# Slab parts, output parts and the last head norm of a gated delta rule's preparation issued later, inside the inverse

## The chip, the cores and the metric

The kernel runs on one core of one Trainium2 chip. The metric is the device time of one execution in microseconds, the median of the runs. All data are fp32; the large projections split each operand into a high and a low fp32r part and add three products.

## The reference

Two blocks of two layers each over 512 tokens and a width of 1024. The change is in the gated delta rule of the first block's two layers (4 heads of 128, here in 4 blocks of 128 tokens):

```python
h = h + 0.5 * swiglu_ffn(rms_norm(h, ffn1_norm[l]), ...)
h = h + hybrid_mixer(...)            # stick-breaking heads beside delta-rule heads
h = h + memory_cross_attention(...)
h = h + 0.5 * swiglu_ffn(...)

# inside the delta rule
decay = where(tril_incl, exp(g[:, None] - g[None, :]), 0)
lower = where(strict, (k*beta) @ k.T * decay, 0)
sol   = triangular_solve(lower + eye, concat([v*beta, k*beta*exp(g)]))
u, w  = split(sol)
qk    = where(tril_incl, q @ k.T * decay, 0)
# scan over the blocks: v_new = u - w @ state; o = q_dec @ state + qk @ v_new; ...
```

The output of the stick-breaking heads is normed per head (`sb_out_norm`) and, beside the delta rule's output, is the input of the output projection.

## The kernel before

Work is a list of stages. Each engine has one program, written out by hand; engines meet only at semaphores. `Mixer` is the stage in question and runs twice, once in each layer of the first block. It has three stretches.

First, the stick-breaking heads in pairs, mixed with the projection slabs of the delta rule. A slab is a weight tile of 128x2048 that DMA brings to `slab_raw`; ScalarE rounds it to `slab_hi` (`k.high`, L277), VectorE takes the rest to `slab_lo` (`k.low`, L284). Head norms are "items": `square(j)` on ScalarE, `sum_item(j)` on TensorE (L1425), `log(j)` (L1671) and `root(j)` (L1676) on ScalarE with a table load ahead of each, `norm(j)` on VectorE (L1869). Item 11 is the norm of the last pair. `high(i)` (L1681, `x_hi`) and `low(i)` (L1875, `x_lo`) split the four output parts for the output projection.

Second, the preparation of the delta rule, a block of 128 tokens (c = 0 to 3) at a time:

- `tensor_rows(c)`: three groups of four matmuls: keys by queries (L1503), the row of gate sums (L1510), the row of betas (L1515).
- `vector_rows(c)`: k times beta (L1944), then the gate difference in four parts (L1949). `scalar_rows(c)`: two exponentials (L1768, L1770). GpSimd masks the decay (L1355).
- `tensor_products(c)`: keys and values turned (L1525, L1528), keys by k-beta (L1535). `scalar_keep(c)`: eight scaled copies of the turned keys, to `k_beta_g` and `k_to_end` (L1781). `vector_products(c)`: five instructions of 128x512 (L1963, L1964, L1966, L1968, L1971), the last makes `inverse_t`, called dt.
- `tensor_turn_d(c)` turns dt (L1544), `scalar_d(c)` copies it out (L1787).

Blocks use PSUM banks 4 to 7 and 0 to 3 by turns (`base(c)`), so `tensor_rows(c)` waits for the readers of block c-2.

Third, the inverse in six levels (`tensor_invert`, `vector_invert`), each for four blocks: first products (L1559), masked on VectorE (L1985); second products (L1565), subtracted on VectorE (L1989); but for the last level, turned again (L1572) and copied by ScalarE (`scalar_turned`, L1794). After it comes the scan over the blocks. Names that the queues below carry: `gdn_qkv` holds queries, keys and values, later the masked and turned matrices; `h_squares`/`gdn_z` are scratch and the gate.

Before the change ScalarE and VectorE have the slab's two parts, the four output parts and item 11 between the blocks of the preparation.

Of the kernel before, what the change touches and what calls it, by code (L numbers as in the profile page):

```python
# [12 lines left out]
P = 128  # L13
# [1208 lines left out]
class Mixer(Stage):  # L1222
# [95 lines left out]
    def item(self, j):  # L1318

        kind, n = ITEMS[j]  # L1320
        data = self.o[:, n, :] if kind == "o" else self.raw[:, (0 if kind == "q" else 4) + n, :]
        batch = [b.index(j) for b in self.BATCH if j in b]
        return data, self.squares[:, j % 6, :], self.k.ps[:, 3 + batch[0] if batch else 2, :]

# [36 lines left out]
    def tensor(self, pe):  # L1361
# [113 lines left out]
        for c in range(TB):  # L1475
            if c + 1 < TB:
                self.tensor_rows(pe, c + 1)
            self.tensor_products(pe, c)
            if c == 0:
                sum_item(11)  # L1480
            if c >= 1:
                self.tensor_turn_d(pe, c - 1)
        self.tensor_turn_d(pe, TB - 1)
        self.tensor_invert(pe)
        self.tensor_scan(pe)
# [33 lines left out]
    def tensor_products(self, pe, c):  # L1519
# [27 lines left out]
    def blocks(self, a, b, odd):  # L1547
        return a.rearrange("p (q two b) -> p q two b", two=2, b=b)[:, :, odd, :]

    def tensor_invert(self, pe):  # L1550
        nc, H = self.k.nc, GD_HEADS
        pe.wait_ge(*self.kept.at(TB))
        pe.wait_ge(*self.vb_kept.at(TB))
        pe.wait_ge(*self.dec_ready.at(TB))
        for n, b in enumerate(self.levels):
            for c in range(TB):
                pe.wait_ge(*self.d_copied.at(n * TB + (c if n else max(c, 2)) + 1))
                for h in range(H):
                    mm = nc.tensor.matmul(self.bank(4 + c)[:, h, :], self.lt[:, c * H + h, :], self.heads(0, c)[:, h, :],  # L1559
                                          start=True, stop=True)  # L1560
                mm.then_inc(self.m1_ready.sem, 1)
# [73 lines left out]
    def scalar(self, act):  # L1635
# [97 lines left out]
        self.scalar_rows(act, 2)  # L1733
        self.scalar_keep(act, 1)
        self.scalar_d(act, 0)
        high(3)
        self.scalar_rows(act, 3)
        self.scalar_keep(act, 2)
        self.scalar_d(act, 1)
        self.scalar_keep(act, 3)  # L1740
        self.scalar_d(act, 2)
        self.scalar_d(act, 3)
        self.scalar_turned(act, 0)
        nc.scalar.activation(self.z, self.z, ACT.Silu).then_inc(self.z_silu.sem, 1)
# [26 lines left out]

    def scalar_keep(self, act, c):
        nc, g = self.k.nc, self.gates
        keys, values, kk, kq = self.base(c)
        act.wait_ge(*self.turned.at(c + 1))
        if c == 0:
            act.wait_ge(*g.bg_ready.at(1))
        for to, bank, col in ((self.kbg, keys, g.bg), (self.kend, keys, g.kend)):
            for h in range(GD_HEADS):
                u = c * GD_HEADS + h  # L1780
                ins = nc.scalar.activation(to[:, u, :], self.bank(bank)[:, h, :], ACT.Copy, scale=col[:, u:u + 1])  # L1781
        ins.then_inc(self.kept.sem, 1)

# [14 lines left out]
    def vector(self, dve):  # L1798
# [130 lines left out]
        self.vector_rows(dve, 2)  # L1929
        self.vector_products(dve, 1)  # L1930
        norm(11)
        self.vector_rows(dve, 3)
        self.vector_products(dve, 2)
        low(2)
        self.vector_products(dve, 3)
        low(3)
        self.vector_invert(dve)
        self.vector_scan(dve)
# [33 lines left out]

    def vector_invert(self, dve):
        k, nc, H = self.k, self.k.nc, GD_HEADS
# [6 lines left out]
        for n, b in enumerate(self.levels):  # L1981
            mask = k.c("levels", (n + 1) * P, P).unsqueeze(1).broadcast_to([P, H, P])
            for c in range(TB):
                dve.wait_ge(*self.m1_ready.at(n * TB + c + 1))
                nc.vector.tensor_tensor(self.heads(4, c), self.bank(4 + c), mask, ALU.mult).then_inc(self.m1_masked.sem, 1)  # L1985
            for c in range(TB):
                dve.wait_ge(*self.p_ready.at(n * TB + c + 1))
                a = halves(self.of(self.dt, c), b, 1)
                nc.vector.tensor_tensor(a, a, close(self.bank(c), b), ALU.subtract).then_inc(self.updated.sem, 1)  # L1989
            if n in (3, 4):  # L1990
                dve.wait_ge(*self.mem_hi_ready.at(1))
                for c in range(4 * n - 12, 4 * n - 8):
                    ins = nc.vector.scalar_tensor_tensor(out=self.mem_lo[:, c, :], in0=self.mem[:, c, :],
                                                         scalar=self.mem_gain[:, c:c + 1],
                                                         in1=self.mem_hi[:, c, :].bitcast(F32),
                                                         op0=ALU.mult, op1=ALU.subtract)
        ins.then_inc(self.mem_split.sem, 1)

# [904 lines left out]
```

## Time and profile before

| | us |
|---|---|
| median of 3 runs | 3319.66 (3318.96 to 3319.77) |
| the profiled execution | 3322.68 |
| its span | 3320.6 |
| PE busy | 3257.4 (98%) |
| PE weight loads busy | 2683.8 (81%) |
| DVE busy | 1664.3 (50%) |
| ACT busy | 1342.0 (40%) |
| POOL busy | 147.4 (4%) |

PE is TensorE, DVE VectorE, ACT ScalarE, POOL GpSimd, SP the engine that issues the DMAs. Each fp32 matmul stands in the trace as two records, so four matmuls of the program read x8. Matmul records overlap: a group's cost in a stream is the distance from its start to the next group's start. "idle ... <-" names what ended the wait. A mixer's preparation lies near 590 to 622 us in the first layer and near 1853 to 1885 us in the second.

### The profile page before, as it was taken

How to read it: one execution, taken by the hardware profiler on the slowest of the kernel's cores; microseconds unless marked ns; L12 is line 12 of the kernel's file. 1: busy time of each engine (PE TensorE's matmuls, PEld its weight loads, DVE VectorE, ACT ScalarE, POOL GpSimd, SP SyncE). 2: the span in 40 equal slices, each digit the busy share in tenths (PEclk: the TensorE clock that was granted, in tenths of full speed). 3: DMA queues.
4: the chain of work that ended last, by engine and by line, in shares of the span. 5: the costliest groups of instructions: out<-in, count | busy, mean ns of one | idle time of the engine just before them, and what ended most of it. 6: DMA issues, size and time to landing. Idle time of an engine off the chain costs nothing.

```text
span 3320.6 us, 39177 instructions
## 1 busy us (share of the span) xinstructions
PE 3257.4 (98%) x16640; PEld 2683.8 (81%) x16640; DVE 1664.3 (50%) x2280; ACT 1342.0 (40%) x1735; POOL 147.4 (4%) x176
## 2 busy tenths in 40 slices
PE   8999999899999999999999899999999999999999
PEld 7888887898688888888887798688888886888767
DVE  5443358654544434443348655444434457543574
ACT  5222248533432223222338643332224446453463
POOL 0000001100000000000001200000000004000040
PEclk9999999999999999999999999999999999999999
DMA  4222221022122222222221113122222220222102
GB/s 162 100 94 90 99 83 55 26 91 100 51 91 100 90 96 106 91 100 88 103 77 64 39 54 112 51 102 90 97 91 107 77 79 24 75 97 89 64 21 88
DMA packets 46893, 275.03 MB, mean 83 GB/s; under 512 B 5248, under 2 KB 8576, under 8 KB 21504
## 3 DMA queue, kind: packets, MB, share of 16 engines
q1 hardware_dynamic: 46720, 272.53, 23.0%
q8 instruction: 132, 2.16, 0.3%
q14 instruction: 41, 0.34, 0.0%
HBM read 270.41 MB, written 2.10 MB: 82 GB/s over the span
## 4 chain that ended last, share of the span: by engine, by line
PE 93%; DVE 3%; ACT 2%; issue 1%; DMA 0%; SPq 0%; ACTq 0%; DVEq 0%
PE banks L295 78%; PE banks L1559 1%; PE banks L1389 1%; PE banks L2747 1%; PE banks L1565 1%; PE banks L2418 1%; PE banks L2430 1%; PE banks L2216 1%; PE banks L1002 1%; ACT slab_hi L277 1%; DVE slab_lo L284 1%; PE banks L1425 1%; PE banks L1572 1%; PE banks L1086 0%; PE banks L1374 0%
## 5 line engine op out<-in xcount | busy, mean ns | idle before, releaser
L295 PE MATMUL banks<-x_hi,slab_hi 128*128 128x512 f32 x2688 | 1061.1, 395 | 12.0 <-DVE x_lo L376 11.6
L295 PE MATMUL banks<-x_hi,slab_lo 128*128 128x512 f32 x2688 | 1048.4, 390 | 0.0
L295 PE MATMUL banks<-x_lo,slab_hi 128*128 128x512 f32 x2688 | 1048.0, 390 | 0.0
L277 ACT ACTIVATE slab_hi<-slab_raw 128x2048 fp32r<-128x2048 f32 (+2 forms) x276 | 483.7, 1753 | 1037.3 <-PE banks L295 1024.1
L284 DVE TENSOR_TENSOR slab_lo<-slab_raw,slab_hi 128x2048 fp32r<-128x2048 f32 (+2 forms) x276 | 577.3, 2092 | 425.1 <-ACT slab_hi L277 425.1
L295 PEld LDWEIGHTS banks<-x_hi,slab_hi 128*128 128x128 f32 x2688 | 505.4, 188 | 123.4 <-issue 18.7
L295 PEld LDWEIGHTS banks<-x_lo,slab_hi 128*128 128x128 f32 x2688 | 505.5, 188 | 108.9 <-issue 5.7
L295 PEld LDWEIGHTS banks<-x_hi,slab_lo 128*128 128x128 f32 x2688 | 505.1, 188 | 105.7
L295 PE MATMUL banks<-hidden_hi,slab_lo 128*128 128x512 f32 x704 | 274.2, 389 | 0.0
L295 PE MATMUL banks<-hidden_hi,slab_hi 128*128 128x512 f32 x704 | 274.2, 389 | 0.0
L295 PE MATMUL banks<-hidden_lo,slab_hi 128*128 128x512 f32 x704 | 274.2, 389 | 0.0
L801 DVE TENSOR_TENSOR hidden<-banks,rstd 128x512 f32<-128x512 f32 x88 | 60.8, 690 | 313.9 <-PE banks L295 313.9
L778 DVE SCALAR_TENSOR_TENSOR h<-banks,h 128x512 f32<-128x512 f32 x80 | 55.1, 689 | 217.8 <-PE banks L295 217.8
L810 ACT ACTIVATE hidden_hi<-hidden 128x512 fp32r<-128x512 f32 x88 | 55.6, 632 | 255.2 <-DVE hidden L818 255.2
L295 PEld LDWEIGHTS banks<-hidden_lo,slab_hi 128*128 128x128 f32 x704 | 132.2, 188 | 27.5
L295 PEld LDWEIGHTS banks<-hidden_hi,slab_hi 128*128 128x128 f32 x704 | 132.2, 188 | 27.4
L295 PEld LDWEIGHTS banks<-hidden_hi,slab_lo 128*128 128x128 f32 x704 | 132.2, 188 | 27.3
L295 PE MATMUL banks<-slab_hi,x_hi 128*128 128x256 f32 x384 | 112.4, 293 | 0.0
L295 PE MATMUL banks<-slab_hi,x_lo 128*128 128x256 f32 x384 | 108.8, 283 | 0.0
L295 PE MATMUL banks<-slab_lo,x_hi 128*128 128x256 f32 x384 | 108.8, 283 | 0.0
L2454 POOL TENSOR_SCALAR weights<-weights,row_scale 128x128 f32<-128x128 f32 (+1 forms) x64 | 85.5, 1341 | 480.2 <-DVE row_scale L2513 480.2
L807 ACT ACTIVATE silu_gate<-silu_gate 128x512 f32<-128x512 f32 x88 | 55.7, 632 | 117.8 <-DVE silu_gate L801 117.7
(362 smaller groups left out, 3984.0 us busy)
## 6 DMA issues: line engine op xcount, KB each, us to landing
slab_raw<-slabs SPq DMA_DIRECT2D x196, 1024.0 KB, 4.8
slab_raw<-slabs SPq DMA_DIRECT2D x64, 704.0 KB, 4.0
slab_raw<-slabs SPq DMA_DIRECT2D x16, 640.0 KB, 3.9
h<-xT SPq DMA_DIRECT2D x8, 256.0 KB, 5.6
memory<-memT SPq DMA_DIRECT2D x2, 1024.0 KB, 5.2
out<-h SPq DMA_DIRECT2D x8, 256.0 KB, 4.3
constants<-con SPq DMA_DIRECT2D x1, 1412.5 KB, 10.2
memory_in<-memT SPq DMA_DIRECT2D x1, 1024.0 KB, 14.6
```

What stands on the lines that cost most here:

```text
L277: self.nc.scalar.activation(self.wh[:, g % self.HIGHS, 0:w], self.raw[:, g % self.RAWS, 0:w], ACT.Copy).then_inc(self.hi_ready, 1)
L284: self.nc.vector.tensor_tensor(self.wl[:, g % self.RAWS, 0:w], self.raw[:, g % self.RAWS, 0:w], self.wh[:, g % self.HIGHS, 0:w].bitcast(F3 ...
L295: mm = self.nc.tensor.matmul(out, left[a], right[c], start=start and n == 0, stop=stop and n == 2)
L778: k.nc.vector.scalar_tensor_tensor(out=h, in0=k.ps[:, jobs[n].bank, :], scalar=self.scale, in1=h, op0=ALU.mult, op1=ALU.add).then_inc(k.ba ...
L801: k.nc.vector.tensor_tensor(to, k.ps[:, jobs[n].bank, :], k.rstd[:], ALU.mult).then_inc(k.bank_free, 1)
L807: k.nc.scalar.activation(a, a, ACT.Silu).then_inc(k.act_done, 1)
L810: k.nc.scalar.activation(self.hh[:, i, :], self.hid[:, i % 2, :], ACT.Copy).then_inc(k.hh_ready, 1)
L1002: mm = nc.tensor.matmul(ps[:, 4 + c, :], self.k.c("heads64"), self.buf(p)[:, c, :], start=True, stop=True)
L1389: mm = nc.tensor.matmul(sc[:, to:to + n], (self.tail if j == b else self.full)[:], part[:, at:at + n], start=False, stop=True, skip_group_ ...
L1425: nc.tensor.matmul(bank, k.c("heads64") if ITEMS[j][0] == "o" else k.ones[:], sq, start=True, stop=True) \
L1559: mm = nc.tensor.matmul(self.bank(4 + c)[:, h, :], self.lt[:, c * H + h, :], self.heads(0, c)[:, h, :], start=True, stop=True)
L2454: ins = self.k.nc.gpsimd.tensor_scalar(w, w, self.col(self.ri, tb, 1), None, ALU.mult)
```

## The change

On ScalarE and VectorE the slab's parts, the four output parts and item 11 move out of the preparation to places in the inverse's first two levels (VectorE's inverse is cut into calls by level for this). On TensorE item 11's sum moves from behind block 0's products to behind the first products of level 0; level 0's first products of blocks 0 and 1 come before the fourth block's dt is turned, with waits of their own by bank. On ScalarE `scalar_keep` is cut in two, with a copy of the previous block's dt between the halves, and each block's exponentials come after the previous block's copies.

The end of the preparation on TensorE, where L1544 turns a dt and L1559 are the first products of level 0. Before:

```order
L1535 MATMUL banks<-k_beta,gdn_qkv 128x128 x4
L1544 MATMUL banks<-constants,inverse_t 128x128 x4
L1525 MATMUL banks<-constants,gdn_qkv 128x128 x4
L1528 MATMUL banks<-constants,gdn_qkv 128x128 x4
L1535 MATMUL banks<-k_beta,gdn_qkv 128x128 x4
L1544 MATMUL banks<-constants,inverse_t 128x128 x8
L1559 MATMUL banks<-gdn_qkv,l_transposed 128x128 x16
L1565 MATMUL banks<-inverse_t,gdn_qkv 128x64 x16
```

After (L1546 turns, L1565 are first products, L1582 second products, L1425 is item 11's sum):

```order
L1537 MATMUL banks<-k_beta,gdn_qkv 128x128 x4
L1546 MATMUL banks<-constants,inverse_t 128x128 x4
L1565 MATMUL banks<-gdn_qkv,l_transposed 128x128 x8
L1546 MATMUL banks<-constants,inverse_t 128x128 x4
L1565 MATMUL banks<-gdn_qkv,l_transposed 128x128 x8
L1425 MATMUL banks<-head_squares,constants 128x512
L1582 MATMUL banks<-inverse_t,gdn_qkv 128x64 x16
```

Eight first products now stand ahead of the last turn, and the sum of item 11 behind the other eight.

VectorE from block 0's rows on, before:

```order
L1880 COPY sb_out<-banks 128x512
L284 TENSOR_TENSOR slab_lo<-slab_raw,slab_hi 128x2048
L1944 TENSOR_TENSOR k_beta<-banks,gdn_qkv 128x512
L1949 TENSOR_SCALAR decay<-banks,gdn_gc 128x128 x4
L1963 TENSOR_TENSOR l_transposed<-banks,decay 128x512
L1964 TENSOR_TENSOR decay<-banks,decay 128x512
L1966 TENSOR_TENSOR inverse_t<-l_transposed,constants 128x512
L1968 TENSOR_TENSOR v_beta<-banks,gdn_beta 128x512
L1971 TENSOR_TENSOR inverse_t<-constants,inverse_t 128x512
L1875 TENSOR_TENSOR x_lo<-sb_out,x_hi 128x512 x2
L1944 TENSOR_TENSOR k_beta<-banks,gdn_qkv 128x512
```

And after, in the first two levels of the inverse (L2003 masks, L2007 subtracts):

```order
L2003 TENSOR_TENSOR gdn_qkv<-banks,constants 128x4x128 x4
L2007 TENSOR_TENSOR inverse_t<-inverse_t,banks 128x128x2 x4
L1889 SCALAR_TENSOR_TENSOR sb_out<-sb_out,params,head_squares 128x512
L1895 TENSOR_TENSOR x_lo<-sb_out,x_hi 128x512 x3
L2003 TENSOR_TENSOR gdn_qkv<-banks,constants 128x4x128 x4
L2007 TENSOR_TENSOR inverse_t<-inverse_t,banks 128x64x4 x4
L1895 TENSOR_TENSOR x_lo<-sb_out,x_hi 128x512
L284 TENSOR_TENSOR slab_lo<-slab_raw,slab_hi 128x2048
L2003 TENSOR_TENSOR gdn_qkv<-banks,constants 128x4x128 x4
```

All that stood between the blocks on VectorE now stands behind level 0 and level 1.

ScalarE after, from the last block's copies to the third level (L1800 are the scaled copies, L1807 copies dt, L1814 the turned matrices, L1763 is the gate):

```order
L1800 ACTIVATE k_to_end<-banks,gdn_kend 128x128 x4
L1682 ACTIVATE head_squares<-sb_out 128x512
L1807 ACTIVATE gdn_qkv<-banks 128x4x128
L1688 ACT_TABLE_LOAD
L1688 ACTIVATE head_squares<-banks 128x512
L1693 ACT_TABLE_LOAD
L1693 ACTIVATE head_squares<-head_squares 128x512
L1698 ACTIVATE x_hi<-sb_out 128x512 x3
L1814 ACTIVATE gdn_qkv<-banks 128x4x128 x4
L1698 ACTIVATE x_hi<-sb_out 128x512
L277 ACTIVATE slab_hi<-slab_raw 128x2048
L1763 ACT_TABLE_LOAD
```

Three output parts, item 11's two table loads and its two functions now stand ahead of level 0's four turned copies, the slab's high part behind them.

The diff, cut to its core (`vector_invert` is otherwise the same code for one level n):

```diff
 # tensor
             self.tensor_products(pe, c)
-            if c == 0:
-                sum_item(11)
             if c >= 1:
                 self.tensor_turn_d(pe, c - 1)
+        for c in range(2):
+            self.tensor_off_diagonal(pe, 0, c)
         self.tensor_turn_d(pe, TB - 1)
+        for c in range(2, TB):
+            self.tensor_off_diagonal(pe, 0, c)
+        pe.wait_ge(*self.dec_ready.at(TB))
+        sum_item(11)
         self.tensor_invert(pe)
 # tensor_products
-        if c == 1:
-            pe.wait_ge(*self.logged.at(12))
-        elif c >= 2:
+        if c >= 2:
             pe.wait_ge(*self.d_copied.at(c - 1))
+    def tensor_off_diagonal(self, pe, n, c):
+        if n == 0 and c == 0:
+            pe.wait_ge(*self.kept.at(3))
+        elif n == 0 and c == 1:
+            pe.wait_ge(*self.vb_kept.at(3))
+        elif n == 0 and c == 2:
+            pe.wait_ge(*self.d_copied.at(3))
+        elif n == 0:
+            pe.wait_ge(*self.dec_ready.at(3))
+        pe.wait_ge(*self.d_copied.at(n * TB + c + 1))
+        for h in range(GD_HEADS):
+            mm = self.k.nc.tensor.matmul(self.bank(4 + c)[:, h, :], self.lt[:, c * GD_HEADS + h, :],
+                                         self.heads(0, c)[:, h, :], start=True, stop=True)
+        mm.then_inc(self.m1_ready.sem, 1)
 # tensor_invert
-        pe.wait_ge(*self.kept.at(TB))
-        pe.wait_ge(*self.vb_kept.at(TB))
-        pe.wait_ge(*self.dec_ready.at(TB))
                 pe.wait_ge(*self.m1_masked.at(n * TB + c + 1))
+                if n == 0 and c < 2:
+                    pe.wait_ge(*(self.kept, self.vb_kept)[c].at(TB))
+                elif n == 0:
+                    pe.wait_ge(*(self.d_copied.at(TB) if c == 2 else self.logged.at(12)))
 # scalar
         self.scalar_rows(act, 0)
-        for i in range(2):
-            high(i)
+        self.scalar_rows(act, 1)
+        for c in range(2):
+            self.scalar_keep(act, c, 0)
+            self.scalar_keep(act, c, 1)
+            if c:
+                self.scalar_d(act, 0)
+            self.scalar_rows(act, c + 2)
+        self.scalar_keep(act, 2, 0)
+        self.scalar_d(act, 1)
+        self.scalar_keep(act, 2, 1)
+        self.scalar_keep(act, 3, 0)
+        self.scalar_d(act, 2)
+        self.scalar_keep(act, 3, 1)
         square(11)
-        k.high(act, self.g0 + SB_HEADS + 1)
-        high(2)
-        self.scalar_rows(act, 1)
-        self.scalar_keep(act, 0)
+        self.scalar_d(act, 3)
         log(11)
         root(11)
...
+        for i in range(3):
+            high(i)
+        self.scalar_turned(act, 0)
         high(3)
...
+        k.high(act, self.g0 + SB_HEADS + 1)
 # vector
-        k.low(dve, self.g0 + SB_HEADS + 1)
-        self.vector_rows(dve, 1)
-        self.vector_products(dve, 0)
-        for i in range(2):
-            low(i)
...
+        for c in range(TB):
+            if c + 1 < TB:
+                self.vector_rows(dve, c + 1)
+            self.vector_products(dve, c)
+        self.vector_invert(dve, 0)
+        norm(11)
+        for i in range(3):
+            low(i)
+        self.vector_invert(dve, 1)
+        low(3)
+        k.low(dve, self.g0 + SB_HEADS + 1)
+        for n in range(2, len(self.levels)):
+            self.vector_invert(dve, n)
```

## Rows read from the trace of the kernel before

**Rows 1.** The page, part 4: the chain that ended last, shares of the span.
```profile
PE 93%; DVE 3%; ACT 2%; issue 1%; DMA 0%; SPq 0%; ACTq 0%; DVEq 0%
```

**Rows 2.** Windows, preparations: length, PE, PEld, DVE, ACT, POOL busy, PEclk, DMA, GB/s.
```profile
590.50:622.00 31.50, 22.09 (x157) 20.23 (x156) 23.49 (x42) 21.63 (x52) 10.37 (x19) 0.86 0.10 34
1853.50:1885.00 31.50, 22.09 (x156) 20.22 (x156) 23.49 (x42) 21.59 (x52) 10.37 (x19) 0.86 0.10 34
```

**Rows 3.** Timeline, TensorE, first mixer: start us, us, what, [idle before <- releaser].
```profile
592.38 1.06 PE L1515 MATMUL banks<-constants,gdn_beta 128*128 128x128 f32 x8
...
599.25 1.85 PE L1503 MATMUL banks<-gdn_qkv 128*128 128x128 f32 x8 [3.19 <-DVE decay L1964]
600.89 1.96 PE L1510 MATMUL banks<-constants,gate_g 128*128 128x128 f32 x8
602.65 1.20 PE L1515 MATMUL banks<-constants,gdn_beta 128*128 128x128 f32 x8
...
607.47 1.16 PE L1503 MATMUL banks<-gdn_qkv 128*128 128x128 f32 x8 [1.42 <-DVE decay L1964]
...
616.07 1.62 PE L1535 MATMUL banks<-k_beta,gdn_qkv 128*128 128x128 f32 x8 [1.95 <-ACT gdn_qkv L1787]
...
621.03 1.09 PE L1544 MATMUL banks<-constants,inverse_t 128*128 128x128 f32 x4 [2.49 <-DVE inverse_t L1971]
621.91 6.09 PE L1559 MATMUL banks<-gdn_qkv,l_transposed 128*128 128x128 f32 x32
627.84 3.69 PE L1565 MATMUL banks<-inverse_t,gdn_qkv 128*128 128x64 f32 x32
631.36 1.91 PE L1572 MATMUL banks<-constants,inverse_t 128*128 128x128 f32 x16
633.11 3.74 PE L1559 MATMUL banks<-gdn_qkv,l_transposed 128*128 128x128 f32 x32
...
636.68 3.69 PE L1565 MATMUL banks<-inverse_t,gdn_qkv 128*128 128x64 f32 x32
```

**Rows 4.** Timeline, VectorE, the same stretch.
```profile
594.07 2.29 DVE L284 TENSOR_TENSOR slab_lo<-slab_raw,slab_hi 128x2048 fp32r<-128x2048 f32 x1 [2.77 <-ACT slab_hi L277]
596.28 0.68 DVE L1944 TENSOR_TENSOR k_beta<-banks,gdn_qkv 128x512 f32<-128x512 f32 x1
596.89 1.11 DVE L1949 TENSOR_SCALAR decay<-banks,gdn_gc 128x128 f32<-128x128 f32 x4
...
603.89 0.69 DVE L1944 TENSOR_TENSOR k_beta<-banks,gdn_qkv 128x512 f32<-128x512 f32 x1 [1.67 <-PE banks L1515]
...
611.09 0.69 DVE L1944 TENSOR_TENSOR k_beta<-banks,gdn_qkv 128x512 f32<-128x512 f32 x1 [1.19 <-PE banks L1515]
...
617.80 0.69 DVE L1963 TENSOR_TENSOR l_transposed<-banks,decay 128x512 f32<-128x512 f32 x1 [1.13 <-PE banks L1535]
```

**Rows 5.** Timeline, ScalarE, the same stretch.
```profile
592.15 1.89 ACT L277 ACTIVATE slab_hi<-slab_raw 128x2048 fp32r<-128x2048 f32 x1
...
602.65 1.28 ACT L1676 ACT_TABLE_LOAD   x1
603.95 0.63 ACT L1676 ACTIVATE head_squares<-head_squares 128x512 f32<-128x512 f32 x1
...
606.79 1.12 ACT L1781 ACTIVATE k_beta_g<-banks,gdn_bg 128x128 f32<-128x128 f32 x4
607.79 1.15 ACT L1781 ACTIVATE k_to_end<-banks,gdn_kend 128x128 f32<-128x128 f32 x4
...
632.00 2.06 ACT L1794 ACTIVATE gdn_qkv<-banks 128x512 f32<-128x512 f32 x4 [9.24 <-PE banks L1572]
```

**Rows 6.** Windows in the first preparation, columns as in rows 2.
```profile
599.30:603.00 3.70, 3.70 (x18) 3.70 (x19) 2.92 (x5) 3.65 (x9) 0.91 (x2) 0.54 0.00 0
...
607.00:611.00 4.00, 3.16 (x26) 2.97 (x27) 2.90 (x5) 3.50 (x11) 1.43 (x4) 1.00 0.00 0
...
621.00:628.00 7.00, 6.96 (x38) 7.00 (x39) 2.56 (x4) 0.60 (x1) 0.00 (x0) 0.58 0.01 2
```

More of the change, by code:

```diff
@@ L1322, in item @@
         batch = [b.index(j) for b in self.BATCH if j in b]
-        return data, self.squares[:, j % 6, :], self.k.ps[:, 3 + batch[0] if batch else 2, :]
+        return data, self.squares[:, j % 6, :], self.k.ps[:, 3 + batch[0] if batch else 3, :]
     def head(self, a, c):
@@ L1548, in blocks @@
         return a.rearrange("p (q two b) -> p q two b", two=2, b=b)[:, :, odd, :]
+    def tensor_off_diagonal(self, pe, n, c):
[12 more added lines that the diff above has]
+        mm.then_inc(self.m1_ready.sem, 1)
     def tensor_invert(self, pe):
         nc, H = self.k.nc, GD_HEADS
-        pe.wait_ge(*self.kept.at(TB))
-        pe.wait_ge(*self.vb_kept.at(TB))
-        pe.wait_ge(*self.dec_ready.at(TB))
         for n, b in enumerate(self.levels):
             for c in range(TB):
[L1557 to L1561, printed above, removed]
+                if n:
+                    self.tensor_off_diagonal(pe, n, c)
             for c in range(TB):
                 pe.wait_ge(*self.m1_masked.at(n * TB + c + 1))
+                if n == 0 and c < 2:
+                    pe.wait_ge(*(self.kept, self.vb_kept)[c].at(TB))
+                elif n == 0:
+                    pe.wait_ge(*(self.d_copied.at(TB) if c == 2 else self.logged.at(12)))
                 for h in range(H):
@@ L1770, in scalar_rows, with scalar_keep @@
         nc.scalar.activation(self.of(self.dec, c), self.of(self.dec, c), ACT.Exp).then_inc(self.dec_exp.sem, 1)
-    def scalar_keep(self, act, c):
+    def scalar_keep(self, act, c, part):
         nc, g = self.k.nc, self.gates
-        keys, values, kk, kq = self.base(c)
         act.wait_ge(*self.turned.at(c + 1))
-        if c == 0:
+        if c == 0 and part == 0:
             act.wait_ge(*g.bg_ready.at(1))
[L1778 to L1782, printed above, removed]
+        to, col = (self.kend, g.kend) if part else (self.kbg, g.bg)
+        for h in range(GD_HEADS):
+            u = c * GD_HEADS + h
+            ins = nc.scalar.activation(to[:, u, :], self.bank(self.base(c)[0])[:, h, :], ACT.Copy, scale=col[:, u:u + 1])
+        if part:
+            ins.then_inc(self.kept.sem, 1)
     def scalar_d(self, act, c):
@@ L1923, in vector @@
         copy_out(self.PAIRS - 1)
-        k.low(dve, self.g0 + SB_HEADS + 1)
-        self.vector_rows(dve, 1)
-        self.vector_products(dve, 0)
-        for i in range(2):
-            low(i)
[L1929 to L1937, printed above, removed]
+        for c in range(TB):
[8 more added lines that the diff above has]
+        low(3)
+        k.low(dve, self.g0 + SB_HEADS + 1)
+        for n in range(2, len(self.levels)):
+            self.vector_invert(dve, n)
         self.vector_scan(dve)
@@ L1971, in vector_products, with vector_invert @@
         nc.vector.tensor_tensor(dt, ident, dt, ALU.subtract).then_inc(self.dt_ready.sem, 1)
-    def vector_invert(self, dve):
-        k, nc, H = self.k, self.k.nc, GD_HEADS
+    def vector_invert(self, dve, n):
+        k, nc, H, b = self.k, self.k.nc, GD_HEADS, self.levels[n]
         def halves(a, b, odd):
@@ L1980, in close @@
             return a[:, :, 0:P // 2].rearrange("p h (q b) -> p h q b", b=b)
[L1981 to L1996, printed above, removed]
@@ L1997, in vector_invert @@
-        ins.then_inc(self.mem_split.sem, 1)
+        mask = k.c("levels", (n + 1) * P, P).unsqueeze(1).broadcast_to([P, H, P])
+        for c in range(TB):
+            dve.wait_ge(*self.m1_ready.at(n * TB + c + 1))
+            nc.vector.tensor_tensor(self.heads(4, c), self.bank(4 + c), mask, ALU.mult).then_inc(self.m1_masked.sem, 1)
+        for c in range(TB):
+            dve.wait_ge(*self.p_ready.at(n * TB + c + 1))
+            a = halves(self.of(self.dt, c), b, 1)
+            nc.vector.tensor_tensor(a, a, close(self.bank(c), b), ALU.subtract).then_inc(self.updated.sem, 1)
@@ new lines, in vector_invert @@
+        if n in (3, 4):
+            dve.wait_ge(*self.mem_hi_ready.at(1))
+            for c in range(4 * n - 12, 4 * n - 8):
+                ins = nc.vector.scalar_tensor_tensor(out=self.mem_lo[:, c, :], in0=self.mem[:, c, :],
+                                                     scalar=self.mem_gain[:, c:c + 1],
+                                                     in1=self.mem_hi[:, c, :].bitcast(F32),
+                                                     op0=ALU.mult, op1=ALU.subtract)
+            if n == 4:
+                ins.then_inc(self.mem_split.sem, 1)
```

10 lines of the change are left out of this document (removed).

## The prediction

> **What bounds the kernel now.** I read the chain of waits first, then busy time by stretch, then the timelines of the three engines side by side. The chain is TensorE for 93% of the span [rows 1], so over most of the kernel only less or faster TensorE work would help. The two preparations are different: in each 31.50 us stretch PE is busy 22.09 us, DVE 23.49, ACT 21.61, none of them full, and the mean granted clock is 0.86 [rows 2]. The two stretches agree to 0.05 us in every column, so I work out the first and count it twice.
>
> The timelines say what the time goes to. PE stands still 3.19, 1.42, 1.95 and 2.49 us, released by DVE or ACT each time [rows 3]. DVE in turn waits for PE, and once 2.77 us for `slab_hi`, after which `slab_lo` takes 2.29 us, and only then does block 1's k-beta start, at 596.28 [rows 4]; PE had its input ready at 592.38 + 1.06 = 593.44 [rows 3]. It is a ring: rows on PE, k-beta and difference on DVE, exponential and scaled copies on ACT, and the banks given back to PE. What stands in the ring beside the blocks' own work is paid in full. The inverse is the opposite: from one level's second products to the next's it takes 636.68 - 627.84 = 8.84 us, made of first products 3.57, second 3.52 and turns 1.75, PE without a gap [rows 3].
>
> The clock is a second loss. After the 3.19 us stop the groups L1503 and L1510 take 1.64 and 1.76 us (599.25 to 600.89 to 602.65), where a group of four 128x128 takes 0.89 in the inverse (3.57/4); the stretch has 0.54 of the clock, near the 1.2 GHz level. Level 0's first products take 5.93 us (621.91 to 627.84) against 3.57 in level 1, at 0.58 [rows 3, 6]. Around the 1.42 us stop the clock stayed at 1.00, the 2.4 GHz level [rows 3, 6].
>
> **The change, term by term, for one mixer.** Nothing is removed but waits. I follow the starts of k-beta (L1944) on DVE.
>
> Term 1, the slab's two parts leave the way to block 1: k-beta goes from 596.28 to 593.44 less a hand-over, -2.9 us.
>
> Term 2, the ring from block 1 to block 2 is now k-beta 0.6 (596.28 to 596.89), difference 1.11 [rows 4], exponential 0.54 (its like is at 603.95, 0.63 long), eight scaled copies 1.00 + 1.15 (606.79, 607.79) [rows 5], PE's two row groups 0.89 + 1.06 [rows 3], five hand-overs of some 0.05: 6.6 us. Before it was 603.89 - 596.28 = 7.61 [rows 4], with item 11's loads and functions in ACT's part and 2.96 instead of 1.96 us for the row groups at the low clock (600.89 to 603.85). -1.0 us.
>
> Term 3, block 2 to block 3: the same 6.6 instead of 611.09 - 603.89 = 7.20. -0.6 us.
>
> Term 4, block 3's k-beta to level 0's second products. Before: 611.09 to 627.84, 16.75 us. Now: (a) k-beta by keys, L1535, waits for dt 1's copy, which stands one group of scaled copies earlier, so it starts 4.0 instead of 4.98 us after k-beta (616.07 - 611.09): -1.0. (b) L1535 at the high clock takes 1.1 instead of the 1.73 us that pass to DVE's L1963 at 617.80: -0.7. (c) DVE's five instructions to the turn's start keep their 3.2 us (617.80 to 621.03). (d) Then 6.81 us passed (621.03 to 627.84): the turn 0.88 and sixteen first products 5.93. Eight of these now fill PE's wait for dt 3; behind it remain the turn 0.44, eight products 1.78 and item 11's sum. The sum has the columns of one group of four (128x512), 0.89, the value I take; it was hidden in a stop of PE before and is now on the path. 3.1 instead of 6.81: -3.7. Together -5.4.
>
> The sum is -9.9 us per mixer, level 0's second products at about 617.9 on the old scale. Two mixers: -19.8.
>
> Where the moved work goes. ACT stood idle 9.24 us before level 0's turned copies at 632.00 [rows 5]. Ahead of them now stand two loads 1.28 each, log 0.60, root 0.63 and three parts at 0.54: 5.4 us. The log cannot start before the sum, about 618.0. That gives root's end at 620.9, the parts' end at 622.5 and the first copy finished at 623.1, against level 1's first products at 617.9 + 3.52 + 1.75 = 623.2. It fits, with 0.1 us to spare, so this is the place to watch. Banks: the last second products wait for the log, done near 618.7, needed at 620.6. Behind the copies come one part 0.54, slab part 1.9 [rows 5] and the gate's load and pass, 3.2 together (1.28 and, being 128x2048 like the slab, 1.9), to about 630.1; level 1's copies are wanted at 631. It fits by about 1 us. DVE has eight instructions per level of at most 128x512; at 0.61 each (596.28 to 596.89) that is at most 4.9 of 8.84 us [rows 4]. Level 0 adds the norm and three parts, four times 0.6, 2.4; level 1 adds 0.6 and 2.29. The first mask can be taken up from 0.9 us after the level's first product and must be done, 0.7 long, by 3.57: it may start 1.9 us late, and what comes between the last subtraction and that point, some 2 us of turns and first product, is free before. Both hide, so 0; if they did not, 5.3 us per mixer. POOL and the DMA queue are passed by nothing: the memory's load on SP still hangs on the fourth block's turned values, which come earlier.
>
> A price that the trace bears on directly is the table load. The row shows 1.28 us and the next activation 0.02 us behind it (602.65 + 1.28 to 603.95) [rows 5]. The Trainium skill, "ScalarE: Activation LUTs", section "What ACT_TABLE_LOAD costs", says a switch costs some 1.38 us more for a drain. By that, two switches would put ACT's copies 2.8 us later and the whole 2.7 us later a mixer, 5.3 for both; by the row, nothing. The row decides.
>
> Bounds. A sum at 0.44, if its second pass overlapped, would give 0.9 us back for both mixers; hand-overs and the ends of pipelined groups are read to about 0.1 us in some 12 steps a mixer, so the gain could be up to 1.2 us a mixer larger: low end 3299.9 - 0.9 - 2.4 = 3296.6.
>
> The profiled execution has 3322.68 us, 2.1 above its span and 3.0 above the median of 3319.66. From it: 3302.9. From the median, which I forecast: 3299.9.
>
> **Rivals.**
>
> Cold first stretch. The clock is the assumption. New stops of PE, by my steps: about 1.5 and 0.6 us before block 2's rows (about 595 to 598), 1.1 and 0.6 before block 3's, 1.2 before the last L1535, 1.1 before the last turn. The longest is close to the 1.42 us stop that kept the clock, but the 1.95 us one was followed by slow groups [rows 3, 6]. If the clock falls at block 2's rows the ring there costs 1.0 to 1.4 us as before: +2.4 for both, 3302.3. For it: the first two stops lie within about 3 us; against: all are shorter than 1.95.
>
> Cold to the end. If PE runs all of the preparation's slow places slowly again, terms 2, 4b and 4d lose 1.0, 0.7 and 2.8 us: +4.5 a mixer, 3308.9.
>
> ACT late in the inverse. If ACT's queue ahead of the turned copies is over 0.1 us longer than I have it, level 1 waits by the excess, and the gate's pass can do the same to level 2. A delay like one more load (1.28) in each: +2.6 for one level, +5.2 for both: 3302.5 to 3305.1. By the drain that the Trainium skill's page on ScalarE states it would be 3305.2.
>
> Only the first stall goes. If the ring is held by something that I take for hidden (GpSimd's mask, say) the blocks keep their 7.6 and 7.2 and term 4 its length: 2 x 2.9, 3313.9. Against: DVE waited for PE or ACT there, never for GpSimd. This is also the case in which the change does little of what it says.
>
> Slower. The inverse is the one stretch in which PE never stops. If no moved work hides there, ACT's 5.4 + 0.54 + 1.9 = 7.8 and DVE's 5.3 us are added in full, 13.1 against 9.9 gained: +3.2 a mixer, 3326.1. It decides from the point where ACT's late copies hold level 1 and DVE's slab part holds level 2, one after the other, for more than 9.9 us. Against: 9.24 us idle on ACT, at least 3.9 a level on DVE.
>
> **How the numbers follow.** All warm and hidden 50%, 3299.9 (own range 3296.6 to 3302). Cold first stretch 20%, 3302.3. Cold to the end 12%, 3308.9. ACT late 12%, 3302.5 to 3305.1. First stall only 4%, 3313.9. Slower 2%. Range: from the low bound to the cold case, 3296.6 to 3308.9, which leaves out half of that case and the last two. About 0.2%, 6.6 us, is what a measurement can tell from no change; only the last two fall short of it: faster 94%, same 4%, slower 2%.
>
> **What would show it.** In the new profile: block 1's k-beta about 5 us after block 0's; the three k-betas 6.6 us apart; no row group over 1.1 us; PE's stops four to six of at most 1.5 us; granted clock 1.00 from 595 us on; sixteen first products in two parts with the last turn between; level 0's second products 25.5 us after block 1's row of betas starts (592.38 before, 617.9 by my steps) and level 1's first products without a stop before them; 8.84 us per level throughout. It would be wrong if a level is longer, if PE waits for L1814's copies, or if the clock row shows 0.5 after 595.

## The result and the profile after

The changed kernel takes 3302.25 us (median of 5, 3301.78 to 3304.35) against 3319.77 us: ratio 0.9946, interval 0.9931 to 0.9960. Forecast were 3299.9 us, a range of 3296.6 to 3308.9, and faster. The profiled execution spans 3300.5 us (3302.44 us with what lies around it) against 3320.6.

Parts 1 and 4 of the page of the changed kernel, TensorE's busy time and the chain; TensorE is busy 11.2 us less though it does the same products:

```profile
PE 3246.2 (98%) x16640; PEld 2674.5 (81%) x16640; DVE 1663.8 (50%) x2280; ACT 1342.0 (41%) x1735; POOL 145.3 (4%) x176
...
PE 94%; DVE 3%; ACT 2%; issue 1%; DMA 0%; SPq 0%; DVEq 0%; ACTq 0%
```

The stretches that answer to [rows 2], columns as there (the second mixer starts 8.5 us earlier now):

```profile
590.50:622.00 31.50, 26.81 (x223) 24.48 (x219) 22.36 (x45) 18.83 (x49) 9.33 (x20) 1.00 0.11 36
1843.50:1875.00 31.50, 26.80 (x221) 24.27 (x217) 22.66 (x46) 18.42 (x48) 9.73 (x20) 1.00 0.13 43
```

The granted clock is 1.00 instead of 0.86, and PE is busy 4.7 us more of the same 31.50 us: since the preparation is shorter, the window now takes in more of the inverse. The timeline of TensorE that answers to [rows 3]; L1507, L1514 and L1519 are the old L1503, L1510 and L1515, and L1537, L1546, L1565, L1582, L1589 the old L1535, L1544, L1559, L1565, L1572:

```profile
591.50 1.16 PE L1507 MATMUL banks<-gdn_qkv 128*128 128x128 f32 x8
...
597.65 1.16 PE L1507 MATMUL banks<-gdn_qkv 128*128 128x128 f32 x8 [1.44 <-DVE decay L1983]
599.01 1.13 PE L1514 MATMUL banks<-constants,gate_g 128*128 128x128 f32 x8 [0.21 <-ACT k_to_end L1800]
...
604.25 1.16 PE L1507 MATMUL banks<-gdn_qkv 128*128 128x128 f32 x8 [1.01 <-DVE decay L1983]
605.60 1.13 PE L1514 MATMUL banks<-constants,gate_g 128*128 128x128 f32 x8 [0.20 <-ACT k_to_end L1800]
...
611.62 1.16 PE L1537 MATMUL banks<-k_beta,gdn_qkv 128*128 128x128 f32 x8 [0.92 <-ACT gdn_qkv L1807]
612.80 0.63 PE L1546 MATMUL banks<-constants,inverse_t 128*128 128x128 f32 x4
613.26 1.95 PE L1565 MATMUL banks<-gdn_qkv,l_transposed 128*128 128x128 f32 x16
616.12 0.63 PE L1546 MATMUL banks<-constants,inverse_t 128*128 128x128 f32 x4 [0.91 <-DVE inverse_t L1990]
616.58 2.07 PE L1565 MATMUL banks<-gdn_qkv,l_transposed 128*128 128x128 f32 x16
618.49 1.02 PE L1425 MATMUL banks<-head_squares,constants 128*128 128x512 f32 x2
619.35 3.68 PE L1582 MATMUL banks<-inverse_t,gdn_qkv 128*128 128x64 f32 x32
622.87 1.92 PE L1589 MATMUL banks<-constants,inverse_t 128*128 128x128 f32 x16
624.62 3.74 PE L1565 MATMUL banks<-gdn_qkv,l_transposed 128*128 128x128 f32 x32
628.19 3.68 PE L1582 MATMUL banks<-inverse_t,gdn_qkv 128*128 128x64 f32 x32
```

Six stops of at most 1.44 us stand where [rows 3] have four of 1.42 to 3.19; the prediction had 1.5, 0.6, 1.1, 0.6, 1.2 and 1.1, and they came as 1.44, 0.21, 1.01, 0.20, 0.92 and 0.91. No group is slow: L1507 and L1514 start 1.36 us apart with a stop between them. VectorE, answering to [rows 4]:

```profile
594.48 0.69 DVE L1963 TENSOR_TENSOR k_beta<-banks,gdn_qkv 128x512 f32<-128x512 f32 x1 [2.17 <-PE banks L1519]
...
601.07 0.69 DVE L1963 TENSOR_TENSOR k_beta<-banks,gdn_qkv 128x512 f32<-128x512 f32 x1 [1.61 <-PE banks L1519]
...
607.66 0.69 DVE L1963 TENSOR_TENSOR k_beta<-banks,gdn_qkv 128x512 f32<-128x512 f32 x1 [1.61 <-PE banks L1519]
...
612.88 0.69 DVE L1982 TENSOR_TENSOR l_transposed<-banks,decay 128x512 f32<-128x512 f32 x1 [0.23 <-PE banks L1537]
...
625.88 1.43 DVE L2003 TENSOR_TENSOR gdn_qkv<-banks,constants 128x512 f32<-128x512 f32 x2
...
635.06 1.98 DVE L2003 TENSOR_TENSOR gdn_qkv<-banks,constants 128x512 f32<-128x512 f32 x3
```

The k-betas (L1963) stand 6.59 us apart both times. Behind the moved norm and output parts VectorE takes up level 1's masks (L2003) at 625.88, behind the slab's low part those of level 2 at 635.06. TensorE's second products start at 628.19 and 637.04 all the same, 8.84 and 8.85 us after the level before: the moved work is hidden. ScalarE, answering to [rows 5]:

```profile
617.40 1.28 ACT L1688 ACT_TABLE_LOAD   x1
619.55 0.60 ACT L1688 ACTIVATE head_squares<-banks 128x512 f32<-128x512 f32 x1 [0.87 <-PE banks L1425]
620.16 1.28 ACT L1693 ACT_TABLE_LOAD   x1
621.46 0.63 ACT L1693 ACTIVATE head_squares<-head_squares 128x512 f32<-128x512 f32 x1
622.00 1.66 ACT L1698 ACTIVATE x_hi<-sb_out 128x512 fp32r<-128x512 f32 x3
623.56 2.04 ACT L1814 ACTIVATE gdn_qkv<-banks 128x512 f32<-128x512 f32 x4
...
632.36 2.06 ACT L1814 ACTIVATE gdn_qkv<-banks 128x512 f32<-128x512 f32 x4 [1.22 <-PE banks L1589]
```

The second table load ends at 621.44 and the root starts at 621.46. Level 0's turned copies (L1814) start at 623.56 and level 1's first products at 624.62, which is where TensorE's turns end: nothing waits.

From here on "the stretch" is the time from TensorE's first group behind the last pair's product of weights and values (L1404; the group starts at 590.49 us before, 591.50 after) to level 1's first products (633.11 and 624.62). Each is read from one profiled execution, to 0.02 us; whole executions of one kernel differ by up to 6.5 us.

| kernel | stretch, mixer 1 and 2 | span less both | median | ratio to before (interval) |
|---|---|---|---|---|
| before | 42.62, 42.63 | 3235.4 | 3319.77 | |
| changed | 33.12, 33.13 | 3234.3 | 3302.25 | 0.9946 (0.9931 to 0.9960) |
| slab parts only | 39.65, 38.19 | 3236.9 | 3316.40 | 0.9987 (0.9977 to 0.9996) |
| changed, slab back | 35.98, 35.93 | 3235.5 | 3309.20 | 0.9965 (0.9952 to 0.9978) |
| changed, turn first | 36.42, 36.12 | 3232.8 | 3307.61 | 0.9962 (0.9947 to 0.9977) |
| changed, item 11 back | 35.53, 35.39 | 3233.1 | 3305.97 | 0.9957 (0.9940 to 0.9973) |
| before with fillers | 39.74, 40.76 | 3234.4 | 3317.77 | 0.9993 (0.9984 to 1.0002) |
| changed, copies uncut | 34.17, 34.17 | 3235.5 | 3305.90 | 0.9952 (0.9939 to 0.9966) |
| sum early | 32.28, 32.28 | 3234.8 | 3301.27 | 0.9937 (0.9924 to 0.9951) |
| ring shortened | 30.95, 30.95 | 3235.4 | 3299.01 | 0.9930 (0.9917 to 0.9942) |
| values first | 29.31, 29.32 | 3233.7 | 3294.39 | 0.9925 (0.9913 to 0.9938) |
| changed, again | 33.12, 33.13 | 3233.8 | 3304.12 | 0.9951 (0.9937 to 0.9965) |

Each ratio is against before on the same chip, whose medians were 3319.74 to 3321.71 (single executions 3317.97 to 3323.23).

### The profile page after: what moved, and what is told of

Its sections match the earlier page's. It is cut to its first block, busy times and chain, and to the rows that moved or that the text cites. A ratio compares the mean times of both kernels' runs of the same rounds, so it can differ in the third digit from the quotient of the medians.

```text
span 3300.5 us, 39191 instructions
## 1 busy us (share of the span) xinstructions
PE 3246.2 (98%) x16640; PEld 2674.5 (81%) x16640; DVE 1663.8 (50%) x2280; ACT 1342.0 (41%) x1735; POOL 145.3 (4%) x176
## 4 chain that ended last, share of the span: by engine, by line
PE 94%; DVE 3%; ACT 2%; issue 1%; DMA 0%; SPq 0%; DVEq 0%; ACTq 0%
PE banks L295 78%; PE banks L1389 1%; PE banks L1582 1%; PE banks L2437 1%; PE banks L1565 1%; PE banks L2449 1%; PE banks L2766 1%; PE banks L2235 1%; PE banks L1002 1%; PE banks L1425 1%; ACT slab_hi L277 1%; DVE slab_lo L284 1%; PE banks L1404 1%; PE banks L1589 1%; PE banks L1086 0%
```

## The experiments

**Slab parts only.** In the kernel before:

```diff
         square(11)
-        k.high(act, self.g0 + SB_HEADS + 1)
 ...
         self.scalar_turned(act, 0)
+        k.high(act, self.g0 + SB_HEADS + 1)
 # vector: k.low(...) from ahead of vector_rows(dve, 1) to behind level 1
```

> The kernel before, with only the slab's two parts moved into the inverse; output parts, item 11, the order of turns and the uncut scaled copies stay. Theory (ring and clock): block 1's k-beta comes 2.9 us earlier in each mixer, TensorE's 3.19 us stop shrinks to about 0.4, the granted clock stays 1.00 at block 2's rows and they take 1.0 us less on the path; the later stops and the slow first products of level 0 stay. -3.9 us per mixer, -7.8 in all against before. Rival A (only the clock counts, the moved work was hidden anyway): -1.0 per mixer, -2.0. Rival B (only the moved work counts): -2.9 per mixer, -5.8, with the clock still at half after 599 us.

Measured -3.0 and -4.4 us a mixer. The first stop fell to 0.58 us and block 2's rows ran fast, as the theory said. But that gained nothing on the path: block 3's rows start 14.17 us into the stretch in both mixers, 2.81 earlier than before, which is what block 1's k-beta gained alone. The next stop grew from 1.42 to 2.44 us instead, and in the first mixer the clock fell there. TensorE at block 3's rows:

```profile
604.37 1.21 PE L1503 MATMUL banks<-gdn_qkv 128*128 128x128 f32 x8 [2.44 <-DVE decay L1967]
605.89 2.07 PE L1510 MATMUL banks<-constants,gate_g 128*128 128x128 f32 x8 [0.31 <-ACT k_to_end L1781]
607.76 1.54 PE L1515 MATMUL banks<-constants,gdn_beta 128*128 128x128 f32 x8
609.13 0.60 PE L1525 MATMUL banks<-constants,gdn_qkv 128*128 128x128 f32 x4
```

The row groups, 0.9 us each elsewhere, take 1.87 and 1.37 us; in the second mixer of the same execution they take 0.9. One program, two lengths of the same stretch: behind the same 2.44 us stop the clock fell once and held once. The theory's -3.9 lies between the two mixers, but not by its sum: the 1.0 us at block 2's rows is not in it, and level 0's first products took 4.87 and 4.67 us instead of 5.93. Rival B's -2.9 is the first mixer's number by chance, since its condition (slow rows behind 599 us) did not hold; rival A's -1.0 is out.

**The slab back in the changed kernel.** `k.high` ahead of block 1's exponentials, `k.low` ahead of block 1's rows, out of the inverse.

> The changed kernel with the slab's two parts back between block 0 and block 1, all else as changed. Theory: block 1's k-beta 2.9 us later, TensorE's stop before block 2's rows 1.4 + 2.9 = 4.3 us, so that the clock falls there and adds 1.0: +3.9 us per mixer, +7.8 against the changed kernel, -10 against before. Rival A (only the clock counts): +1.0 per mixer. Rival B (clock stays up): +2.9 per mixer, +5.8.

Measured +2.86 and +2.80. The stop grew to 2.48 us, not 4.3: ScalarE comes to the slab 0.09 us into the stretch, 1.57 earlier than in the kernel before, where two output parts and item 11's square stand ahead of it. Block 1's k-beta starts at 4.23 us instead of 2.98. The clock did fall behind the stop:

```profile
597.97 1.16 PE L1507 MATMUL banks<-gdn_qkv 128*128 128x128 f32 x8 [2.48 <-DVE decay L1983]
599.49 1.72 PE L1514 MATMUL banks<-constants,gate_g 128*128 128x128 f32 x8 [0.37 <-ACT k_to_end L1800]
601.00 1.92 PE L1519 MATMUL banks<-constants,gdn_beta 128*128 128x128 f32 x8
602.71 0.91 PE L1529 MATMUL banks<-constants,gdn_qkv 128*128 128x128 f32 x4
```

1.51 and 1.71 us for groups of 0.97 and 0.89. So both parts of the theory are there, with other sizes: the work 1.25 us where I had 2.9, the clock 1.36 where I had 1.0, and 0.24 in the next turn of the ring.

**Turn first.**

```diff
-        for c in range(2):
-            self.tensor_off_diagonal(pe, 0, c)
         self.tensor_turn_d(pe, TB - 1)
-        for c in range(2, TB):
+        for c in range(TB):
             self.tensor_off_diagonal(pe, 0, c)
```

> The changed kernel with all sixteen first products of level 0 behind the fourth block's turn. The stop before that turn grows from 0.9 to 2.9 us. Theory: eight products (1.8 us) return to the path, and after such a stop the clock falls as before, so that the first products take 5.9 instead of 3.6 us and the turn 0.4 more: +4.5 us per mixer, +9 against the changed kernel. Rival (the clock holds, since the earlier stops are short now): +1.8 per mixer, +3.6.

Measured +3.30 and +2.99, between the two. TensorE there:

```profile
614.91 0.63 PE L1544 MATMUL banks<-constants,inverse_t 128*128 128x128 f32 x4 [2.70 <-DVE inverse_t L1988]
615.38 5.36 PE L1563 MATMUL banks<-gdn_qkv,l_transposed 128*128 128x128 f32 x32
620.58 1.02 PE L1425 MATMUL banks<-head_squares,constants 128*128 128x512 f32 x2
```

After a stop of 2.70 us sixteen first products take 5.20 us (to item 11's sum at 620.58) instead of 3.57: 1.6 us for the clock, and 1.7 for the order (3.57 instead of the 1.91 that stand behind the turn in the changed kernel). In the kernel before they took 5.93 [rows 3]: there a stop of 1.95 us had come ahead of the 2.49, and the clock was down already when they began.

**Item 11 back.** Square ahead of block 1's rows, sum behind block 0's products, log and root behind block 0's copies, norm behind block 1's products.

> The changed kernel with item 11 back in the preparation (square ahead of block 1's rows on ScalarE, sum behind block 0's products, log and root with their two table loads behind block 0's copies, norm behind block 1's products on VectorE). Theory: ScalarE's 3.8 us lie in the ring between block 0's copies and block 2's exponential, where it has 1.3 us to spare: +2.4 us, and the sum's 0.86 us leaves the end of the preparation: +1.6 per mixer, +3.1 against the changed kernel if the clock holds; with a stop of TensorE of over 2 us in its products the clock may fall there and add about 1 per mixer: +5. Rival (item 11 is hidden there, its sum on the path is what counts): -0.9 per mixer, -1.7.

Measured +2.41 and +2.26. The theory's three parts are there, two with other sizes: block 3's rows start 1.43 us later (14.18 instead of 12.75 us into the stretch; I had 2.4), behind a stop of 2.44 us the two row groups take 3.50 us instead of 1.86 in the first mixer (1.6 for the clock; I had 1), and the sum's 0.86 leaves the path. The rival is out.

**The kernel before with fillers in TensorE's stops.**

```diff
+FILL_A = 12
+FILL_B = 7
...
             if c == 0:
+                pe.wait_ge(*self.o_copied.at(self.PAIRS))
+                for n in range(FILL_A):
+                    nc.tensor.matmul(ps[:, 2, 0:P], k.c("ident"), k.c("ident"), start=True, stop=True)
                 sum_item(11)
...
+        pe.wait_ge(*self.vb_kept.at(3))
+        for n in range(FILL_B):
+            nc.tensor.matmul(ps[:, 5, 0:P], k.c("ident"), k.c("ident"), start=True, stop=True)
         self.tensor_turn_d(pe, TB - 1)
```

> The kernel before with idle matmuls added in two of TensorE's stops of each preparation: 12 of 128x128 (identity by identity, some 2.7 us at the high clock) ahead of item 11's sum, in the 3.19 us stop, and 7 (1.6 us) ahead of the fourth block's turn, in the 2.49 us stop. Their products are thrown away. Nothing else moves. Theory (a part of the change's gain is the clock alone): block 2's rows stay at 2.4 GHz, -1.0 us per mixer; if the clock also holds behind the 1.95 us stop, which stays, the last block's products, turn and level 0's first products give 3.5 more: stretch from block 1's first product to level 1's first product 42.6 to 38.1 us, -9 us in all. If it falls at the 1.95 us stop as before, only -1.0 per mixer or nothing: 41.6 us. Rival (the clock is a symptom, what counts is what the other engines do): 42.6 us, or more by what the added matmuls delay.

Measured 39.74 and 40.76 against 42.6: in the profiled execution (3316.58 us) the stretch with nineteen useless matmuls is 2.9 and 1.9 us shorter. By the median it is 3.9 us, and the ratio 0.9993 (0.9984 to 1.0002) doesn't tell it from nothing: six of its ten executions took 3315.4 to 3318.0 us with a mean granted clock of 0.996 to 0.998, the other four 3320.5 to 3321.9 with 0.995, within before's own 3318.7 to 3322.4. TensorE (L1484 and L1490 are the fillers, L1567 level 0's first products):

```profile
595.41 2.84 PE L1484 MATMUL banks<-constants 128*128 128x128 f32 x24
...
599.62 1.16 PE L1511 MATMUL banks<-gdn_qkv 128*128 128x128 f32 x8 [0.51 <-DVE decay L1972]
601.16 1.16 PE L1518 MATMUL banks<-constants,gate_g 128*128 128x128 f32 x8 [0.37 <-ACT k_to_end L1789]
...
616.47 1.47 PE L1543 MATMUL banks<-k_beta,gdn_qkv 128*128 128x128 f32 x8 [1.96 <-ACT gdn_qkv L1795]
...
618.59 2.68 PE L1490 MATMUL banks<-constants 128*128 128x128 f32 x14
...
621.75 3.74 PE L1567 MATMUL banks<-gdn_qkv,l_transposed 128*128 128x128 f32 x32
```

The first products take 3.57 us (621.75 to 625.32) instead of 5.93, behind the same 1.96 us stop and slow groups after it; the seven fillers took the slow time instead (2.69 us, where seven quarters of 0.89 are 1.56). But block 2's rows, fast now, bought nothing: block 3's rows start 16.99 us into the stretch here, and 16.98 before. The gain went into the stop ahead of them, 2.44 instead of 1.42 us, and in the second mixer the clock fell behind it (row groups of 1.48 and 1.70 us), which is why that mixer won 1.0 us less. VectorE shows why block 2's fast rows bought nothing (L1952 k-beta, L1957 difference):

```profile
603.24 0.69 DVE L1952 TENSOR_TENSOR k_beta<-banks,gdn_qkv 128x512 f32<-128x512 f32 x1 [0.65 <-PE banks L1523]
605.48 1.12 DVE L1957 TENSOR_SCALAR decay<-banks,gdn_gc 128x128 f32<-128x128 f32 x4 [1.54 <-ACT exp_g_row L1776]
```

K-beta is 1.0 us early, then the difference waits 1.54 us for ScalarE's exponential, which stands behind item 11's loads and functions. Item 11 held that turn of the ring, not the clock. In the kernel before, the same wait is 0.52 us, because k-beta itself comes late there:

```profile
605.10 1.13 DVE L1949 TENSOR_SCALAR decay<-banks,gdn_gc 128x128 f32<-128x128 f32 x4 [0.52 <-ACT exp_g_row L1768]
```

**Copies uncut.** `scalar_d(1)` and `scalar_d(2)` behind both halves of blocks 2's and 3's scaled copies.

> The changed kernel with the scaled copies of blocks 2 and 3 uncut: the copy of dt 1 and dt 2 behind both halves instead of between them. Theory: the last k-beta product starts 1.0 us later; VectorE had 0.2 us to spare ahead of its last five instructions: +0.8 us per mixer, the stretch 33.1 to 33.9 us, +1.6 in all. Rival (ScalarE is not what the last product waits for): 33.1.

Measured +1.04 in both mixers. The 0.23 us that VectorE stood idle ahead of its last five instructions was a wait for the very product that moved, no reserve. The stop ahead of that product is 1.96 us here, and the granted clock stayed 1.00 in both stretches.

The four parts undone one by one cost 2.83, 3.15, 2.34 and 1.04 us (means of the two mixers), 9.4 of the 9.50 gained. That the sum closes is in part chance. Three of the four prices hold 1.3 to 1.6 us of clock that a stop of over 2.4 us brought, and the slab's work is 1.25 us here but 2.8 beside the output parts and the square, as its own run shows. The output parts were not tried alone: the 1.57 us by which ScalarE came to the slab earlier without two of them and the square is their price with the slab in place, and nothing here gives it without.

**Sum early.**

```diff
+        pe.wait_ge(*self.dec_ready.at(TB))
+        sum_item(11)
         self.tensor_turn_d(pe, TB - 1)
         for c in range(2, TB):
             self.tensor_off_diagonal(pe, 0, c)
-        pe.wait_ge(*self.dec_ready.at(TB))
-        sum_item(11)
```

(and `square(11)` ahead of block 1's rows)

> The changed kernel with item 11's sum ahead of the fourth block's turn instead of behind the last first products, and its square on ScalarE ahead of block 1's rows (in a 1.9 us wait), so that the sum's input is there. Theory: the sum's 0.86 us fills the 0.91 us stop before that turn and leaves the path: the stretch 33.1 to 32.3 us, -1.7 in all against the changed kernel. Rival (the sum costs nothing where it is, hidden by masks or the log): 33.1.

Measured -0.84 and -0.85.

**Ring shortened.** Keys by queries (`kq`) leave `tensor_rows` for a place behind `tensor_turn_d`; on ScalarE:

```diff
-            self.scalar_keep(act, c, 0)
-            self.scalar_keep(act, c, 1)
-            ...
-            self.scalar_rows(act, c + 2)
+            self.scalar_keep(act, c, 0)
+            self.scalar_rows(act, c + 1, 1)    # the decay's exponential
+            self.scalar_keep(act, c, 1)
+            ...
+            self.scalar_rows(act, c + 2, 0)    # the row's exponential
```

> As the run with the early sum, and the ring itself shortened: TensorE computes each block's keys-by-queries behind the last block's products and turn instead of ahead of the row sums, and ScalarE does the first half of a block's scaled copies before the next block's decay exponential, in its 2.05 us wait for VectorE. Theory (what bounds the preparation now is the ring row sums, k-beta, difference, exponential, second half of the copies): block 1's k-beta 0.9 us earlier, the ring 5.9 instead of 6.59 us: the stretch 32.3 to some 29.5 us, -7.3 in all against the changed kernel. Rival (TensorE's or VectorE's own work bounds it): VectorE's 17 us from block 1's k-beta on are full and the stretch stays above 31.

Measured 30.95: 1.33 us less than with the early sum, where I expected 2.8, and next to the rival's 31. Block 1's k-beta is 0.9 us earlier (2.09 us into the stretch), as expected, but the ring is 6.5 us, not 5.9. Something else ended last. TensorE's row sums:

```profile
598.10 1.13 PE L1513 MATMUL banks<-constants,gate_g 128*128 128x128 f32 x8 [1.83 <-DVE v_beta L1998]
...
604.63 1.13 PE L1513 MATMUL banks<-constants,gate_g 128*128 128x128 f32 x8 [1.41 <-DVE v_beta L1998]
```

Their releaser is v-beta (L1998), VectorE's fourth product of the block two back, which frees a bank that only the next group, the row of betas, needs.

**Values first.** v-beta of blocks 0 to 2 ahead of the other four products, its wait on TensorE moved from the row sums to the row of betas:

```diff
-            pe.wait_ge(*self.vb_kept.at(c - 1))
 ...
         mm.then_inc(self.grow_ready.sem, 1)
+        if c >= 2:
+            pe.wait_ge(*self.vb_kept.at(c - 1))
```

> As the run with the shortened ring, with one more step out of it: VectorE takes v-beta of blocks 0 to 2 ahead of the block's other four products instead of fourth, and TensorE waits for it only ahead of the beta row. In the last run the row sums started 1.83 and 1.41 us late, released by v-beta. Theory: ScalarE's second half of the scaled copies releases the row sums now, some 0.9 us earlier for block 2 and 0.8 for block 3, and VectorE is nearly full after that: the stretch 30.95 to 29.3 us, -3.3 us in all. Rival (VectorE's work is what is left, not its order): 30.95, or a little more from block 0's first product being 0.6 us later.

Measured 29.31 and 29.32.

```profile
596.91 1.16 PE L1512 MATMUL banks<-constants,gate_g 128*128 128x128 f32 x8 [1.00 <-ACT k_to_end L1812]
...
602.62 1.16 PE L1512 MATMUL banks<-constants,gate_g 128*128 128x128 f32 x8 [0.56 <-ACT k_to_end L1812]
...
609.77 0.63 PE L1554 MATMUL banks<-constants,inverse_t 128*128 128x128 f32 x4 [0.23 <-DVE inverse_t L2007]
...
615.25 3.69 PE L1590 MATMUL banks<-inverse_t,gdn_qkv 128*128 128x64 f32 x32
...
620.52 3.74 PE L1573 MATMUL banks<-gdn_qkv,l_transposed 128*128 128x128 f32 x32
```

The stops are 1.00 and 0.56 us, released by ScalarE's second half, and the last 0.23; the ring is 5.71 us. So it was VectorE's order and the wait, not its work, and the rival is out. With 3294.39 us against 3304.12 for the changed kernel on the same chip it is the fastest kernel here. How much is the wait's and how much VectorE's new order was not taken apart.

**The changed kernel again.**

> The changed kernel again, beside the others on one chip: the stretch 33.1 us in both mixers, and 0.994 to 0.995 of before. If the stops of TensorE let the clock fall in some executions, one of the two stretches will be 1 to 3 us longer.

33.12 and 33.13 us; the median was 15.6 us under before this time, 17.5 the first. The stretch did not change, and the granted clock was 1.00 in both: no clock fell in it.

## Why the prediction was right

Direction and range held. The mechanism was as stated, with item 11's cost put into the wrong term and two terms a little too large.

Term 1: block 1's k-beta starts 2.98 us into the stretch (594.48 - 591.50) instead of 5.79: -2.8, forecast -2.9. The forecast took 0.05 us for a hand-over off the new start where it belongs on it. That the slab did this is shown by the run that moved it alone, with k-beta at 2.98 us. Moved back by itself it puts k-beta at 4.23 us, not at 5.79, since the output parts and the square are no longer ahead of it.

Term 2: 7.61 to 6.59 us, -1.0 as forecast. Of the two reasons given the clock is the right one: with the fillers, item 11 still in its place, the same step takes 6.58 us. Item 11 is not in this term.

Term 3: 7.20 to 6.59, -0.6 as forecast, but no reason was given. It is item 11's: the difference behind block 2's k-beta waits 0.52 us for the exponential that stands behind item 11 on ScalarE. The two terms hang together, which the forecast did not say. With the clock up and item 11 in place, by fillers or by the slab's move, the wait is 1.54 us, and block 3's rows come no earlier for it.

Term 4: 16.75 to 11.69 us (607.66 to 619.35), -5.1 against -5.4. (a) 3.96 us to the last product, -1.0 as forecast, and the uncut copies confirm it (1.04). (b) 1.26 us from there to VectorE, forecast 1.1; -0.5 instead of -0.7. (c) 3.24 us, kept. (d) 3.23 us from the turn to the second products, forecast 3.1: the turn 0.46, eight products 1.91, the sum 0.86. The high value for the sum was right; the early-sum run shows its 0.85 us. Why the eight products take 1.91 us and not 1.78 was not found.

Together -9.50 instead of -9.9 a mixer: -19.0, and 0.8 us of the miss of 2.35. The rest cannot be placed in a trace: the profiled spans differ by 20.1, 1.1 more than the mixers, and the medians by 17.5 and 15.6. The rest of the program took 3232.8 to 3236.9 us in these twelve profiles, 4 us of scatter. The kernel before also has two lengths: of its 38 executions beside the runs above, the 19 with a mean granted clock of 0.993 or 0.994 took 3321.3 to 3323.2 us, the 19 with 0.995 or 0.996 3318.0 to 3321.2. Its only profile, 3322.68 us at 0.993, is of the longer kind, while the median of the result, 3319.77, lies with the shorter. So its 42.6 us stretches are likely on the long side, and the gain of a typical execution smaller than 19.0; no trace of a short execution is here to show where it is shorter.

The rivals. The median, 3302.25 us, is the number of the cold first stretch (3302.3) and lies just outside the own range of the warm case (3296.6 to 3302). The number alone would have picked the wrong case; the rows decide. Cold first stretch and cold to the end: no; stops of 1.44 us and less kept 1.00. ACT late: no; TensorE waits for no copy, with 0.4 us to spare at level 1 (first copy's 0.60 us from 623.56, needed at 624.62) where I had 0.1. The terms given add up to the root's end at 620.5, not 620.9, which is nearly all of that difference. Behind the loads the rows show no drain: 0.02 us from the load's end to the root. So the price that the Trainium skill states ("ScalarE: Activation LUTs", section "What ACT_TABLE_LOAD costs") doesn't appear here either, and the profile's row was the one to sum with. First stall only and slower: no; levels still take 8.84 us (619.35 to 628.19).

## What to carry to other kernels

Find the ring that hands banks from engine to engine, and take out of it, on every engine, what the next lap doesn't need; put it where one engine is full and the others are not. Price each step by undoing it alone, and read in each run where the time went: here four parts added up to the whole within 0.2 us, but partly through losses of clock that only the undoing brought, and one part had another price beside the others. A faster step can end as a longer stop: block 2's rows at the high clock gained nothing while item 11 held the ring. When a step of a shortened ring gives less than its sum, look at the new releaser: a wait set one group of matmuls too early, for a bank needed only by the next group, with its product late in VectorE's order, was worth 0.8 us a lap.

## What the runs showed of the hardware

Useless matmuls can pay. Seven fillers in a stop let the first products behind it run at 2.4 GHz (granted clock 1.00) in both mixers of the profiled execution: 3.57 instead of 5.93 us. Four of that kernel's ten executions were as long as before's, so it is no sure gain.

The clock never fell behind a stop of up to 1.83 us (the shortened ring) in these stretches unless a longer one stood just ahead. Behind stops of 1.95 us and more it sometimes did: behind the 1.95 us stop of the kernel before the granted clock is 0.56 (616 to 621 us), while behind the 1.96 us stops of the run with the uncut copies it stayed 1.00 in both mixers. The same 2.44 us stop in one execution was followed by a group of 1.87 us in one mixer and of 1.00 us in the other.
